# A modulation step moved, sums of squares moved between engines, and two products exchanged in a two-layer diffusion trunk

## The chip, the cores and the metric

The kernel runs on one core of a Trainium2 chip, all in float32. The metric is the device time of one execution in microseconds (us). Five engines run their own instruction streams and meet at semaphores: TensorE (PE: matmuls and transposes, results in PSUM), VectorE (DVE), ScalarE (ACT), GpSimd (POOL, which doesn't touch PSUM here) and SyncE (SP), which only issues DMAs. ACT and POOL issue some DMAs too.

## The reference

One inference step of DEPTH = 2 layers for 512 latent tokens and 128 context tokens, D = 1024. Layer 0 mixes by latent attention and retention, layer 1 by a Conformer convolution; each is followed by a mixture of 32 experts (top 2). Cut to what the change touches:

```
mp, ms = modulation(c_ctx, ...), modulation(c, ...)      # silu(cond) @ ada_w + ada_b, six parts of 1024
# layer 0, end:
xp = xp + mp[5] * hier_moe(hp, ...)                      # 128 context tokens
xs = xs + ms[5] * hier_moe(hs, ...)                      # 512 latent tokens
# layer 1, start:
h = modulate(rms_norm(x, norm_mix), m[0], m[1])          # x * rsqrt(mean(x^2) + eps), then scale and shift
a, g = split(h @ w_in);  u = a * sigmoid(g)
u = depthwise_conv(u, dw, dw_b)                          # 31 taps
u = silu(layer_norm(u, ln_g, ln_b))
x = x + m[2] * (u @ w_out)                               # the output product: 1024 x 1024 weights, 640 tokens
```

## The kernel before, in words

The residual stream lies transposed in SBUF as `xT` (128 partitions x 8 row blocks x 640 tokens). Tokens are cut in five tiles of 128 (`NT` = 5); `TILES` visits the context tile first, then the four latent ones. Nothing plans the order of work: each engine's block in the source is its queue, and semaphores (`ev(name)`) join them.

**End of layer 0 to the start of layer 1.** When the expert outputs are all in HBM (`y_done`), ACT issues five DMAs (L1672) that bring them back as `ygat`, one per tile. In the meantime TensorE multiplies the last eight blocks of modulation weights (`modulation`, L695). Its result leaves PSUM through ACT (`mod_rows(4)`), TensorE turns it in four transposes (`mod_columns(4)`, L684, bank 7), and DVE adds the bias (`mod_bias(4)`, L1754), which raises `mod_c`. These columns hold the gate and the shift that layer 1 uses after its convolution, so nothing of the stage described here reads them; TensorE waits for `mod_c` because a later step writes the same bank.

Then five tiles pass through this row of steps:

- TensorE `combine(s)` (L1201): per half of four row blocks, 4 x 2 products with diagonal weight matrices, 16 matmul instructions a half (each float32 matmul is two instructions). Two halves a tile.
- DVE `residual(s)` (L2281): four instructions a half, added to `xT`; raises `comb`. A bank comes free for `combine` after the half four before.
- ACT squares each half into `hT` (L1436).
- POOL folds the eight row blocks of squares to one in three additions (L2606), for the first four tiles.
- TensorE `tile_sum(s)`: one product with a matrix of ones (L1211), that is two instructions. For the fifth tile the eight blocks are summed by eight products instead (L1216, 16 instructions).
- ACT takes the root (L1443).
- DVE `normed_tile(s)`: reciprocal (L2290), then one product over all eight row blocks (L1754, 128x1024).

The loops of the engines set the lags: TensorE does `combine(s)`, then `tile_sum(s - 2)`; ACT squares tile s, then takes the root of s - 2; DVE does `residual(s)`, then `normed_tile(s - 3)`. After the fifth `normed_tile`, ACT and DVE apply scale and shift, and the gated input product (L1270, 64 instructions of 320 columns for each of 16 parts) begins.

**Output product of layer 1.** `project_out` computes each pair of row blocks by seven products of half size in place of eight (a Strassen scheme): products 1, 2 and 3 read inputs as they are, 5, 6, 7 and 4 read sums of them. `ORDER = (1, 5, 2, 6, 3, 7, 4)`; q = 0, 1 are two column halves of the weights, mt two output blocks in each. Each (product, mt) is a step (`out_step`, 28 a layer) of 4 matmuls, 8 instructions (L762), and raises `wo_mm`. The steps take six banks in turn, so a step waits until DVE has taken the one six before (`take`, L2080, raises `wo_ev`). Product 1 of layer 1 needs `cvn[:, 0:4]`, product 2 `cvn[:, 4:8]`; ACT writes these eight blocks in order (SiLU, L1732), and product 1 of mt 0 waits for them one by one.

The sums of the inputs (`row_sums`) are four DVE instructions over 128x1280 elements (L1754), each with both operands in SBUF, and stand on DVE ahead of every `take`. The sums of the weights are six POOL additions of 128x1024 (`weight_sums`, L2499, L2501, L2502) and, once product 2 of a q is done, one subtraction that overwrites product 2's weights (`last_sum`, L2509), which product 3 then reads.

Of the kernel before, what the change touches and what calls it, by code (L numbers as in the profile page):

```python
# [165 lines left out]
def build(nc, io):  # L166
    f = io
    ctx = ExitStack()
    with ctx:
# [220 lines left out]
        SETUP = 3  # L390
        POOLSET = SETUP + NT - 1
        TURNED = 2 + 2 * NT
# [41 lines left out]
        GATING, ROUTING = 7, 6  # L434
        ORDER = (1, 5, 2, 6, 3, 7, 4)
        SEQ = (0, 1, 4, 5, 2, 3, 6, 7)
# [4 lines left out]

        def out_step(mt, product):

            return 14 * (mt // 2) + 2 * ORDER.index(product) + mt % 2 + 1

        def out_bank(mt, product):

            return (1, 4, 3, 6, 5, 7)[(out_step(mt, product) - 1) % 6]

        def row_done(l, k):  # L450

            return 28 * l + out_step(k % 4, 3 if k < 4 else 4)
        back_full = {}
# [220 lines left out]
        def _(pe):  # L674
# [44 lines left out]
            def project_out(l, x1, x2):  # L719

                kind = ("ev_out", "od_out")[l]
                n0 = 28 * l

                def ready(mt, product):

                    q = mt // 2
                    if out_step(mt, product) > 6:
                        pe.wait_ge(ev("wo_ev"), n0 + out_step(mt, product) - 6)
                    if product in (5, 6, 7):
                        pe.wait_ge(ev("w_sum"), 8 * l + 3 * q + product - 4)  # L730
                        pe.wait_ge(ev("x_sum"), 4 * l + product - 4)
                    if product == 3:
                        pe.wait_ge(ev("w_sum"), 8 * l + 6 + q + 1)
                    if product == 4:
                        pe.wait_ge(ev("x_sum"), 4 * l + 4)
                    if l == 0:
                        if product == 1:
                            pe.wait_ge(ev("ot_v"), NT)
                        if product == 5:
                            pe.wait_ge(ev("o_c"), 6)  # L740
                        if product == 3:
                            pe.wait_ge(ev("octx_c"), 4)
                    elif product == 2:
                        pe.wait_ge(ev("mod_c"), MODC + 6)

                for q in range(2):
                    arrived((kind, q))
                    arrived((kind, 2 + q))
                    w1, w2 = out_weights(l, q), out_weights(l, 2 + q)
                    for product in ORDER:  # L750
                        for mt in (2 * q, 2 * q + 1):
                            ready(mt, product)
                            c = slice(mt % 2 * P, mt % 2 * P + P)
                            for i in range(4):
                                if l == 1 and mt == 0 and product in (1, 2):
                                    pe.wait_ge(ev("ln_sq"), KD + 1 + (0 if product == 1 else 4) + i + 1)
                                left = {1: w1[:, K1[l] + i, c], 2: w1[:, K2[l] + i, c], 3: w1[:, K2[l] + i, c],
                                        4: w2[:, K2[l] + i, c], 5: weight_sum(l, q, 0)[:, i, c],
                                        6: weight_sum(l, q, 1)[:, i, c], 7: w2[:, K1[l] + i, c]}[product]
                                right = {1: x1(i)[:, 0:SEG], 2: x2(i)[:, 0:SEG], 3: x2(i)[:, SEG:T], 4: row_sum[:, 3, i, :],  # L760
                                         5: row_sum[:, 0, i, :], 6: row_sum[:, 1, i, :], 7: row_sum[:, 2, i, :]}[product]
                                last = pe.matmul(PS[:, out_bank(mt, product), 0:SEG], left, right, start=(i == 0), stop=(i == 3))  # L762
                            last.then_inc(ev("wo_mm"), 1)

# [281 lines left out]
            def moe(l):  # L1046
# [136 lines left out]
                if l == 0:  # L1183
                    for n in range(4 * KD, 5 * KD):
                        modulation(n)
                    mod_columns(4)
                    pe.wait_ge(ev("mod_c"), MODC + 5)

# [16 lines left out]
                def tile_sum(s):  # L1205

                    if s >= 2:
                        pe.wait_ge(ev("root"), ROOT[2] + s - 1)
                    if s < NT - 1:
                        pe.wait_ge(ev("h_c"), SETUP + s + 1)  # L1210
                        last = pe.matmul(PS[:, s % 2, 0:P], ones, hT[:, 0, cols(TILES[s])], start=True, stop=True)  # L1211
                    else:
                        for k in range(KD):
                            if k % 4 == 0:
                                pe.wait_ge(ev("squared"), KD + s + 1 + k // 4)
                            last = pe.matmul(PS[:, s % 2, 0:P], ones, hT[:, k, cols(TILES[s])],  # L1216
                                             start=(k == 0), stop=(k == KD - 1))
                    last.then_inc(ev("sumsq"), 1)
# [25 lines left out]
                if l == 1:  # L1244
# [3 lines left out]
                    return  # L1248
                for s in range(NT + 2):
                    if s < NT:  # L1250
                        combine(s)
                    if s >= 2:
                        tile_sum(s - 2)

# [69 lines left out]
        def _(act):  # L1324
# [103 lines left out]
            def norm_tiles():  # L1428

                act.activation(tick[:, 3:4], eps, ACT.Sqrt)  # L1430
                for s in range(NT + 2):
                    if s < NT:
                        for half in range(2):
                            ks = slice(4 * half, 4 * half + 4)
                            act.wait_ge(ev("comb"), 2 * s + half + 1)
                            ins = act.activation(hT[:, ks, cols(TILES[s])], xT[:, ks, cols(TILES[s])], ACT.Square)  # L1436
                            if half == 1 or s == NT - 1:
                                ins.then_inc(ev("squared"), 1)
                    if s >= 2:
                        act.wait_ge(ev("sumsq"), s)  # L1440
                        if s >= 4:
                            act.wait_ge(ev("hn"), HN[2] + s - 3)
                        act.activation(PS[:, 2 + s % 2, 0:P], PS[:, s % 2, 0:P], ACT.Sqrt, bias=eps, scale=1.0 / D) \  # L1443
                            .then_inc(ev("root"), 1)
# [299 lines left out]
        def _(dve):  # L1744
# [299 lines left out]
            def add_square(l, n):  # L2044

                dve.wait_ge(ev("squared"), (KD + NT + 1) * l + n + 1)
                if n >= 2:
# [22 lines left out]
            def add_out(l):  # L2070

                def take(mt, product):

                    dve.wait_ge(ev("wo_mm"), 28 * l + out_step(mt, product))
                    if product != 1:
                        dve.wait_ge(ev("wo_ev"), 28 * l + out_step(mt, product) - 2)
                    for row, n in USES[product]:
                        m = mt + row
                        for c0, c1, who in (((0, SEG, 0),), ((SEG, SAMPLE, 0), (SAMPLE, T, 1)))[n]:
                            last = dve.scalar_tensor_tensor(  # L2080
                                out=xT[:, m, c0:c1], in0=PS[:, out_bank(mt, product), c0 - n * SEG:c1 - n * SEG],
                                scalar=modT[:, l, 16 + m, who:who + 1], in1=xT[:, m, c0:c1], op0=ALU.mult, op1=ALU.add)
                    last.then_inc(ev("wo_ev"), 1)

                for q in range(2):
                    for product in ORDER:
                        for p in range(2):
# [14 lines left out]
            def moe(l):  # L2102
# [164 lines left out]
                with dve.Fori(0, end) as n:  # L2267
                    gate_block(n)
                if l == 0:
                    mod_bias(4)  # L2270

                def residual(s):
# [44 lines left out]
                if l == 1:  # L2317
# [3 lines left out]
                    return  # L2321
                for s in range(NT + 3):
                    if s < NT:
                        residual(s)
                    if s >= 3:
                        normed_tile(s - 3)
                dve.wait_ge(ev("hn"), HN[2] + NT)
# [64 lines left out]
        def _(pool):  # L2392
# [111 lines left out]
            def last_sum(l, q):  # L2504

                a12 = out_weights(l, q)[:, K2[l]:K2[l] + 4, :]
                pool.wait_ge(ev("w_sum"), 8 * l + 6)
                pool.wait_ge(ev("wo_mm"), 28 * l + out_step(2 * q + 1, 2))
                pool.tensor_tensor(a12, a12, weight_sum(l, q, 1), ALU.subtract).then_inc(ev("w_sum"), 1)  # L2509
# [91 lines left out]
            moe(0)  # L2601
            for s in range(NT - 1):
                pool.wait_ge(ev("squared"), KD + s + 1)
                for n in (4, 2, 1):
                    t = cols(TILES[s])
                    ins = pool.tensor_tensor(hT[:, 0:n, t], hT[:, 0:n, t], hT[:, n:2 * n, t], ALU.add)  # L2606
                    if n > 1:
                        link(ins)
                ins.then_inc(ev("h_c"), 1)
            ctx_mod(2)  # L2610
# [79 lines left out]
```

## Time and profile before

| what | us |
|---|---|
| median of 3 runs | 1319.2 (1317.21 to 1320.07) |
| the profiled execution, as timed | 1319.7 |
| its span in the trace | 1317.9 |
| TensorE busy | 1185.1 (90%) |
| DVE / ACT / POOL busy | 606.3 / 380.9 / 434.0 |
| first `combine` to first gated input matmul | 721.09 to 753.45 |
| output product of layer 1, first to last matmul | 943.88 to 1007.40 |

The profile is of one execution. Times in rows are counted from the start of its span. Busy times of an engine say little about what a change is worth; the two stretches of the last lines are where the changed instructions lie.

### The profile page before, as it was taken

The numbers are of one execution on the slowest core, as the hardware profiler recorded it, in microseconds if no ns is written. First come the engines' busy times: TensorE is split into PE (matmuls) and PEld (weight loads), VectorE is DVE, ScalarE is ACT, GpSimd is POOL, SyncE is SP. The second block draws the span as 40 slices with busy tenths as digits, with TensorE's granted clock in tenths as the row PEclk, the third lists the DMA queues.
The fourth block names the chain that finished last, engine by engine and source line by source line (L and its number), as shares of the span: only waits on it lengthen the run. The fifth ranks groups of instructions, "written<-read, shape, count | busy, mean of one in ns | idle before, by whom it ended". The sixth has DMA issues, their size and how long they took to land.

```text
span 1317.9 us, 20755 instructions
## 1 busy us (share of the span) xinstructions
PE 1185.1 (90%) x6709; PEld 746.4 (57%) x6710; DVE 606.3 (46%) x1381; ACT 380.9 (29%) x786; POOL 434.0 (33%) x739
## 2 busy tenths in 40 slices
PE   6999998989999499997786799999799599999884
PEld 5566797555566455553342666666377355555442
DVE  3120344776866522221110739999785422222226
ACT  2120036655522211111110436565514111111111
POOL 0300100340000134443332449997600234444420
PEclk9999999979999799999997899999899799999997
DMA  9775550000053899999997921111763899999976
GB/s 378 267 287 215 210 178 33 3 1 1 1 101 148 349 394 422 423 423 423 424 423 302 301 81 64 64 64 33 196 203 150 316 375 397 384 422 423 422 284 271
DMA packets 107301, 324.76 MB, mean 246 GB/s; under 512 B 23029, under 2 KB 56795, under 8 KB 84707
## 3 DMA queue, kind: packets, MB, share of 16 engines
q1 hardware_dynamic: 86640, 290.38, 57.1%
q0 software_dynamic: 12464, 21.91, 4.7%
q10 hardware_dynamic: 8131, 11.59, 2.5%
q8 instruction: 41, 0.67, 0.2%
q14 instruction: 25, 0.20, 0.0%
HBM read 314.53 MB, written 27.11 MB: 259 GB/s over the span
## 4 chain that ended last, share of the span: by engine, by line
PE 59%; issue 14%; DVE 8%; DMA 7%; POOL 6%; ACT 2%; SPq 2%; POOLq 1%; ACTq 1%; DVEq 0%
PE PS L1270 10%; PE PS L806 9%; PE PS L762 9%; PE PS L1127 8%; PE PS L1149 4%; PE PS L996 3%; POOL arena L2536 2%; PE PS L695 2%; DMA arena<-in_moe_w_down 2%; DVE arena L1754 2%; DMA arena<-in_moe_w_up 2%; DMA ring<-in_ada_w 2%; PE PS L1112 2%; DVE scratch L1754 2%; PE PS L1009 1%
## 5 line engine op out<-in xcount | busy, mean ns | idle before, releaser
L1754 DVE TENSOR_TENSOR arena<-arena,PS 128x128 f32<-128x128 f32 (+3 forms) x109 | 40.2, 385 | 288.8 <-ACT arena L1645 287.6
L1270 PE MATMUL PS<-arena,ring 128*128 128x320 f32 x512 | 141.8, 438 | 7.8 <-issue 6.5
L1127 PE MATMUL PS<-ring,arena 128*64 128x256 f32 x1088 | 131.2, 393 | 16.4 <-DMA ring<-in_moe_w_up 14.7
L2623 POOL TENSOR_TENSOR arena<-arena 128x655 f32<-128x655 f32 x91 | 129.7, 1425 | 42.8 <-ACT arena L1717 30.0
L806 PE MATMUL PS<-ring,arena 128*128 128x256 f32 (+1 forms) x640 | 141.9, 375 | 1.7 <-ACT arena L1457 1.7
L1127 PE MATMUL PS<-arena 128*64 128x256 f32 x1120 | 130.6, 383 | 13.9 <-DMA arena<-in_moe_w_up 12.8
L806 PEld LDWEIGHTS PS<-ring,arena 128*128 128x128 f32 x640 | 115.6, 192 | 28.8 <-issue 14.5
L762 PE MATMUL PS<-arena,ring 128*128 128x320 f32 x448 | 123.8, 439 | 5.1 <-ACT arena L1732 4.8
L1270 PEld LDWEIGHTS PS<-arena,ring 128*128 128x128 f32 x512 | 98.0, 193 | 51.3 <-issue 12.7
L2355 DVE SCALAR_TENSOR_TENSOR PS<-arena,vecT,PS 128x655 f32<-128x655 f32 x124 | 112.1, 904 | 4.2
L1127 PEld LDWEIGHTS PS<-ring,arena 128*64 128x64 f32 x1088 | 77.9, 140 | 59.4 <-DMA ring<-in_moe_w_up 13.3
L762 PEld LDWEIGHTS PS<-arena,ring 128*128 128x128 f32 x448 | 86.3, 193 | 42.6 <-issue 7.6
L1127 PEld LDWEIGHTS PS<-arena 128*64 128x64 f32 x1120 | 78.1, 137 | 55.5 <-DMA arena<-in_moe_w_up 10.9
L1717 ACT ACTIVATE arena<-arena,vecT 128x655 f32<-128x655 f32 x99 | 80.1, 839 | 52.9 <-POOL arena L2623 35.1
L1645 ACT ACTIVATE arena<-PS 128x128 f32<-128x128 f32 x69 | 19.1, 277 | 256.4 <-PE PS L1127 256.4
L1656 ACT ACTIVATE arena<-PS 128x512 f32 x61 | 36.4, 597 | 152.7 <-PE PS L1149 152.7
L2527 POOL TENSOR_TENSOR pool_tick<-cst 128x1 f32<-128x1 f32 x120 | 22.1, 184 | 176.5 <-ACT arena L1656 175.1
L2080 DVE SCALAR_TENSOR_TENSOR xT<-PS,modT,xT 128x320 f32<-128x320 f32 (+2 forms) x176 | 63.1, 421 | 35.6 <-PE PS L762 35.5
L1149 PE MATMUL PS<-arena 128*64 128x512 f32 x280 | 67.8, 605 | 1.5 <-ACT arena L1656 0.8
L1112 PE MATMUL PS<-cst,arena 128*128 128x128 f32 x284 | 53.9, 313 | 16.4 <-DVE arena L2236 16.4
L2536 POOL DMA_INDIRECT arena<-h_rows,gather_col x56 | 59.2, 1058 | 27.6 <-issue 27.6
L2541 POOL DMA_INDIRECT y_rows<-arena,scatter_col x56 | 56.9, 1017 | 32.4 <-issue 32.4
(363 smaller groups left out, 1613.7 us busy)
## 6 DMA issues: line engine op xcount, KB each, us to landing
arena<-in_moe_w_up SPq DMA_DIRECT2D x64, 1024.0 KB, 19.2
ring<-in_moe_w_up SPq DMA_DIRECT2D x64, 1024.0 KB, 15.0
ring<-in_ada_w SPq DMA_DIRECT2D x46, 1024.0 KB, 10.9
arena<-in_moe_w_down SPq DMA_DIRECT2D x32, 1024.0 KB, 20.0
ring<-in_moe_w_down SPq DMA_DIRECT2D x32, 1024.0 KB, 16.3
arena<-y_rows ACTq DMA_DIRECT2D x10, 1024.0 KB, 9.5
ring<-in_od_w_in SPq DMA_DIRECT2D x16, 512.0 KB, 6.2
ring<-in_ev_w_in SPq DMA_DIRECT2D x7, 1024.0 KB, 15.8
```

What stands on the lines that cost most here:

```text
L762: last = pe.matmul(PS[:, out_bank(mt, product), 0:SEG], left, right, start=(i == 0), stop=(i == 3))
L806: last = pe.matmul(z_bank(i)[:, 0:n], hT[:, k, t * P:t * P + P], w[:, k, 0:n], start=(k == 0), stop=(k == KD - 1))
L1112: last = pe.transpose(quad(3)[:, m, :], xrow.rearrange("p (c m) -> p m c", m=4)[:, m, :], ident)
L1127: last = pe.matmul(PS[i * BLK:(i + 1) * BLK, 0, 0:2 * P].rearrange("p (a n) -> p a n", a=2), xblk[:, k, :], w[:, k % 4, :, i * P:(i + 1) * P],
L1149: last = pe.matmul(PS[c * BLK:(c + 1) * BLK, 2, :], hblk[:, i, :], w[:, i, c * 512:(c + 1) * 512], start=(i == 0), stop=(i == 1))
L1270: last = pe.matmul(PS[:, 2 * a + n, 0:SEG], w[:, k, a, :], hT[:, k, n * SEG:(n + 1) * SEG], start=(k == 0), stop=(k == KD - 1))
L1717: act.activation(dst, src, ACT.Copy, scale=tap_weight(w, j)).then_inc(ev("prod"), 1)
L1754: return dve.tensor_tensor(out, a, b, op)
L2080: last = dve.scalar_tensor_tensor(out=xT[:, m, c0:c1], in0=PS[:, out_bank(mt, product), c0 - n * SEG:c1 - n * SEG], scalar=modT[:, l, 16 + ...
L2355: dve.scalar_tensor_tensor(out=conv_acc, in0=src, scalar=tap_weight(w, j), in1=conv_acc, op0=ALU.mult, op1=ALU.add).then_inc(ev("conv_v"), 1)
L2536: pool.indirect_dma_start(land[r], None, h_rows[:, :], bass.IndirectOffsetOnAxis(ap=col, axis=0), bounds_check=2 * T - 1, oob_is_err=False ...
L2623: pool.tensor_tensor(acc, acc, prod[:, i % PRODS, :], ALU.add).then_inc(ev("conv_p"), 1)
```

## The change

Three edits. (a) `mod_columns(4)`, its wait and `mod_bias(4)` move from before `combine(0)` and `residual(0)` to behind them. (b) The POOL additions are gone; ACT announces every half of squares, and TensorE sums all five tiles by eight products each. All lags shorten by one: `tile_sum(s - 1)`, root of s - 1, `normed_tile(s - 2)`. (c) In layer 1 the order of products becomes (1, 2, 5, 6, 3, 7, 4), and for q = 0 products 1 and 2 alternate between mt 0 and 1 after each of the four matmuls. Layer 0 keeps its order. Counts of semaphores follow.

```diff
-        POOLSET = SETUP + NT - 1
+        POOLSET = SETUP
...
-        ORDER = (1, 5, 2, 6, 3, 7, 4)
+        ORDERS = ((1, 5, 2, 6, 3, 7, 4), (1, 2, 5, 6, 3, 7, 4))
...
-                    elif product == 2:
+                    elif product == 5:
                         pe.wait_ge(ev("mod_c"), MODC + 6)
...
-                    for product in ORDER:
-                        for mt in (2 * q, 2 * q + 1):
+                    for product in ORDERS[l]:
+                        pair = (2 * q, 2 * q + 1)
+                        for mt in pair:
                             ready(mt, product)
+                        by_chunk = l == 1 and q == 0 and product in (1, 2)
+                        for n in range(8):
+                            mt, i = (pair[n % 2], n // 2) if by_chunk else (pair[n // 4], n % 4)
...
                 if l == 0:
                     for n in range(4 * KD, 5 * KD):
                         modulation(n)
-                    mod_columns(4)
-                    pe.wait_ge(ev("mod_c"), MODC + 5)
...
-                    if s < NT - 1:
-                        pe.wait_ge(ev("h_c"), SETUP + s + 1)
-                        last = pe.matmul(PS[:, s % 2, 0:P], ones, hT[:, 0, cols(TILES[s])], start=True, stop=True)
-                    else:
-                        for k in range(KD):
-                            if k % 4 == 0:
-                                pe.wait_ge(ev("squared"), KD + s + 1 + k // 4)
-                            last = pe.matmul(PS[:, s % 2, 0:P], ones, hT[:, k, cols(TILES[s])],
-                                             start=(k == 0), stop=(k == KD - 1))
+                    for k in range(KD):
+                        if k % 4 == 0:
+                            pe.wait_ge(ev("squared"), KD + 2 * s + 1 + k // 4)
+                        last = pe.matmul(PS[:, s % 2, 0:P], ones, hT[:, k, cols(TILES[s])],
+                                         start=(k == 0), stop=(k == KD - 1))
...
-                for s in range(NT + 2):
+                for s in range(NT + 1):
                     if s < NT:
                         combine(s)
-                    if s >= 2:
-                        tile_sum(s - 2)
+                    if s == 0:
+                        mod_columns(4)
+                        pe.wait_ge(ev("mod_c"), MODC + 5)
+                    if s >= 1:
+                        tile_sum(s - 1)
...
-                if l == 0:
-                    mod_bias(4)
...
-                for s in range(NT + 3):
+                for s in range(NT + 2):
                     if s < NT:
                         residual(s)
-                    if s >= 3:
-                        normed_tile(s - 3)
+                    if s == 0:
+                        mod_bias(4)
+                    if s >= 2:
+                        normed_tile(s - 2)
...
-                pool.wait_ge(ev("wo_mm"), 28 * l + out_step(2 * q + 1, 2))
+                pool.wait_ge(ev("wo_mm"), 28 * l + out_step(l, 2 * q + 1, 2))
...
-            for s in range(NT - 1):
-                pool.wait_ge(ev("squared"), KD + s + 1)
-                for n in (4, 2, 1):
-                    t = cols(TILES[s])
-                    ins = pool.tensor_tensor(hT[:, 0:n, t], hT[:, 0:n, t], hT[:, n:2 * n, t], ALU.add)
-                    if n > 1:
-                        link(ins)
-                ins.then_inc(ev("h_c"), 1)
             ctx_mod(2)
```

## Rows read from the trace of the kernel before

**Rows 1.** The page: busy time and share of the span of each engine.
```profile
PE 1185.1 (90%) x6709; PEld 746.4 (57%) x6710; DVE 606.3 (46%) x1381; ACT 380.9 (29%) x786; POOL 434.0 (33%) x739
```

**Rows 2.** Chain that ended last: start us, us, what. "issue": no releaser shown.
```profile
719.65 0.20 DVE modT L1754
...
721.09 13.74 PE PS L1201 x96
...
746.98 6.47 issue
753.45 19.55 PE PS L1270 x64
...
774.12 17.46 PE PS L1270 x64
...
951.17 56.23 PE PS L762 x208
```

**Rows 3.** First of the five DMA issues of L1672, issue to landing.
```profile
L1672 ACTq DMA_DIRECT2D arena<-y_rows x1: 392/392/392, 714.1 to 714.1; - x1
...
DMA to landing us min/median/max: 6.9/6.9/6.9
```

**Rows 4.** Timeline 727 to 753: start, length, instruction, [idle before <- releaser].
```profile
727.72 1.12 DVE L2281 SCALAR_TENSOR_TENSOR xT<-PS,modT,xT 128x128 f32<-128x128 f32 x4 [1.71 <-PE PS L1201]
...
729.50 1.13 DVE L2281 SCALAR_TENSOR_TENSOR xT<-PS,modT,xT 128x128 f32<-128x128 f32 x4 [0.66 <-PE PS L1201]
...
734.23 0.63 ACT L1436 ACTIVATE arena<-xT 128x512 f32<-128x512 f32 x1 [1.15 <-DVE xT L2281]
...
734.66 0.39 PE L1211 MATMUL PS<-arena,cst 128*128 128x128 f32 x2
...
736.56 0.32 ACT L1443 ACTIVATE PS<-PS,cst 128x128 f32<-128x128 f32 x1
...
744.92 2.05 PE L1216 MATMUL PS<-arena,cst 128*128 128x128 f32 x16 [1.18 <-ACT PS L1443]
...
748.15 0.96 DVE L2290 RECIPROCAL PS<-PS 128x128 f32<-128x128 f32 x1
...
750.28 0.96 DVE L2290 RECIPROCAL PS<-PS 128x128 f32<-128x128 f32 x1
751.28 1.22 DVE L1754 TENSOR_TENSOR arena<-xT,PS 128x1024 f32<-128x1024 f32 x1
```

**Rows 5.** Windows: length, busy PE, PEld, DVE, ACT, POOL, then PEclk, DMA.
```profile
749.00:751.00 2.00, 0.00 (x0) 0.00 (x0) 1.97 (x3) 0.00 (x0) 0.00 (x0) 0.95 1.03 294
751.00:753.40 2.40, 0.00 (x0) 0.00 (x0) 2.33 (x4) 0.87 (x2) 0.00 (x0) 0.50 1.14 342
...
942.00:943.80 1.80, 0.00 (x0) 0.00 (x0) 1.80 (x5) 0.98 (x2) 1.80 (x2) 0.50 1.02 419
```

**Rows 6.** Timeline of TensorE and POOL at the output product.
```profile
943.88 6.97 PE L762 MATMUL PS<-arena,ring 128*128 128x320 f32 x16 [4.82 <-ACT arena L1732]
...
949.64 3.59 POOL L2502 TENSOR_TENSOR ring<-ring 128x1024 f32<-128x1024 f32 x1
...
960.17 2.36 POOL L2509 TENSOR_TENSOR ring<-ring 128x1024 f32<-128x1024 f32 x1 [6.94 <-PE PS L762]
```

**Rows 7.** Timeline of DVE there: the four row sums, then the first pieces taken.
```profile
948.90 2.12 DVE L1754 TENSOR_TENSOR arena<-arena 128x1280 f32<-128x1280 f32 x1
951.13 3.45 DVE L1754 TENSOR_TENSOR arena<-arena 128x1280 f32<-128x1280 f32 x1
954.50 1.48 DVE L1754 TENSOR_TENSOR arena<-arena 128x1280 f32<-128x1280 f32 x1
955.90 1.48 DVE L1754 TENSOR_TENSOR arena<-arena 128x1280 f32<-128x1280 f32 x1
957.31 0.54 DVE L2080 SCALAR_TENSOR_TENSOR xT<-PS,modT,xT 128x320 f32<-128x320 f32 x1
...
959.39 0.53 DVE L2080 SCALAR_TENSOR_TENSOR xT<-PS,modT,xT 128x320 f32<-128x320 f32 x1
```

More of the change, by code:

```diff
@@ L440, in build, with out_step, out_bank @@
                 3: ((0, 1),), 7: ((4, 0), (4, 1)), 4: ((4, 0),)}
[L442 to L448, printed above, removed]
+        def out_step(l, mt, product):
+            return 14 * (mt // 2) + 2 * ORDERS[l].index(product) + mt % 2 + 1
+        def out_bank(l, mt, product):
+            return (1, 4, 3, 6, 5, 7)[(out_step(l, mt, product) - 1) % 6]
         def row_done(l, k):
-            return 28 * l + out_step(k % 4, 3 if k < 4 else 4)
+            return 28 * l + out_step(l, k % 4, 3 if k < 4 else 4)
         back_full = {}
@@ L726, in ready @@
                     q = mt // 2
-                    if out_step(mt, product) > 6:
-                        pe.wait_ge(ev("wo_ev"), n0 + out_step(mt, product) - 6)
+                    if out_step(l, mt, product) > 6:
+                        pe.wait_ge(ev("wo_ev"), n0 + out_step(l, mt, product) - 6)
                     if product in (5, 6, 7):
@@ L753, in project_out @@
                             c = slice(mt % 2 * P, mt % 2 * P + P)
[L754 to L762, printed above, removed]
@@ L763, in project_out @@
-                            last.then_inc(ev("wo_mm"), 1)
+                            if l == 1 and mt == 0 and product in (1, 2):
+                                pe.wait_ge(ev("ln_sq"), KD + 1 + (0 if product == 1 else 4) + i + 1)
+                            left = {1: w1[:, K1[l] + i, c], 2: w1[:, K2[l] + i, c], 3: w1[:, K2[l] + i, c],
+                                    4: w2[:, K2[l] + i, c], 5: weight_sum(l, q, 0)[:, i, c],
+                                    6: weight_sum(l, q, 1)[:, i, c], 7: w2[:, K1[l] + i, c]}[product]
@@ L765, in _ @@
+                            right = {1: x1(i)[:, 0:SEG], 2: x2(i)[:, 0:SEG], 3: x2(i)[:, SEG:T], 4: row_sum[:, 3, i, :],
+                                     5: row_sum[:, 0, i, :], 6: row_sum[:, 1, i, :], 7: row_sum[:, 2, i, :]}[product]
+                            last = pe.matmul(PS[:, out_bank(l, mt, product), 0:SEG], left, right, start=(i == 0), stop=(i == 3))
+                            if i == 3:
+                                last.then_inc(ev("wo_mm"), 1)
             pe.wait_ge(ev("params_in"), 16 * NPARAM)
@@ L1430, in norm_tiles @@
                 act.activation(tick[:, 3:4], eps, ACT.Sqrt)
-                for s in range(NT + 2):
+                for s in range(NT + 1):
                     if s < NT:
@@ L1435, in norm_tiles @@
                             act.wait_ge(ev("comb"), 2 * s + half + 1)
[L1436 to L1443, printed above, removed]
+                            act.activation(hT[:, ks, cols(TILES[s])], xT[:, ks, cols(TILES[s])], ACT.Square) \
+                                .then_inc(ev("squared"), 1)
+                    if s >= 1:
+                        b = (s - 1) % 2
+                        act.wait_ge(ev("sumsq"), s + 1)
+                        if s >= 3:
+                            act.wait_ge(ev("hn"), HN[2] + s - 2)
+                        act.activation(PS[:, 2 + b, 0:P], PS[:, b, 0:P], ACT.Sqrt, bias=eps, scale=1.0 / D) \
                             .then_inc(ev("root"), 1)
@@ L2044, in add_square @@
             def add_square(l, n):
-                dve.wait_ge(ev("squared"), (KD + NT + 1) * l + n + 1)
+                dve.wait_ge(ev("squared"), (KD + 2 * NT) * l + n + 1)
                 if n >= 2:
@@ L2072, in take @@
                 def take(mt, product):
-                    dve.wait_ge(ev("wo_mm"), 28 * l + out_step(mt, product))
+                    dve.wait_ge(ev("wo_mm"), 28 * l + out_step(l, mt, product))
                     if product != 1:
-                        dve.wait_ge(ev("wo_ev"), 28 * l + out_step(mt, product) - 2)
+                        dve.wait_ge(ev("wo_ev"), 28 * l + out_step(l, mt, product) - 2)
                     for row, n in USES[product]:
@@ L2080, in take @@
                             last = dve.scalar_tensor_tensor(
-                                out=xT[:, m, c0:c1], in0=PS[:, out_bank(mt, product), c0 - n * SEG:c1 - n * SEG],
+                                out=xT[:, m, c0:c1], in0=PS[:, out_bank(l, mt, product), c0 - n * SEG:c1 - n * SEG],
                                 scalar=modT[:, l, 16 + m, who:who + 1], in1=xT[:, m, c0:c1], op0=ALU.mult, op1=ALU.add)
@@ L2085, in add_out @@
                 for q in range(2):
-                    for product in ORDER:
+                    for product in ORDERS[l]:
                         for p in range(2):
```

## The prediction

> **What bounds the kernel now.** I read the page first: TensorE is busy for 90% of the span [rows 1], so work added to it tends to cost, and work taken off other engines tends to give nothing. Then the chain of waits, to see what ends last in the two stretches that the change touches [rows 2]; then their timelines [rows 4, 6, 7], the landing of one DMA [rows 3], and the granted clock at idle gaps [rows 5].
>
> Two things are to be seen in the chain. From 721.09 TensorE's `combine` carries it (96 instructions without a break), and later the end of the stage hangs on DVE's last `normed_tile`, at 751.28 + 1.22 = 752.50; the gated input product starts 0.95 us later, at 753.45. And from 951.17 the output product runs for 56.23 us without a break: 208 instructions, 0.270 us each, 2.16 us per step of eight. So each microsecond by which these two starts move is a microsecond of the kernel; nothing after them shows slack of its own, since each later stage begins with what these release.
>
> **(a) The modulation columns.** Before, the transposes and the bias end at 719.65 + 0.20 = 719.85 [rows 2]. `combine(0)` starts at 721.09. It also needs the first tile of expert outputs: issued at 714.1, landed 6.9 us later, at 721.0 [rows 3]. So the DMA released it, and the columns lay in its shadow for nothing. Moved, they let nothing start earlier. And they gain a price: TensorE now stands after `combine(0)` until DVE has done both halves of `residual(0)` (727.72 + 1.12 = 728.84) [rows 4] and the bias, 0.20, so until about 729.1. Queued behind the wait is `combine(1)`, whose first half before was ready for DVE at 729.50, 1.78 after the last of `combine(0)`; it therefore started about 727.5. Cost: +1.6 us at this point.
>
> **(b) The sums of squares.** A tile sum was two instructions: 0.39 us recorded, about 0.22 of TensorE's time (0.11 an instruction, since a half of 16 takes 1.78) [rows 4]. It becomes 16: the fifth tile's took 2.05 from first start to last end, of which about 1.8 occupy the engine and 0.2 are the last one's way through it. I price each at 1.8. What POOL did was hidden, and an engine that is no bound gives nothing back.
>
> Walk with these prices, 3.58 for a `combine`, 1.1 for half a `residual`, 0.6 for a square, 0.32 for a root, 2.13 for a `normed_tile` (748.15 to 750.28):
>
> - TensorE: `combine(1)` 729.1 to 732.7; sum 0 to 734.5; `combine(2)` to 738.1; sum 1 to 739.9; `combine(3)` to 743.45; sum 2 to 745.25; `combine(4)` to 748.8; sum 3 to 750.6.
> - Each sum finds its squares ready, and DVE's `normed_tile(0)` and `(1)` fit into its idle time (739.4 to 741.5, 744.8 to 746.9) but for sum 4: half a `residual` ends at 750.15, its square at 750.8, the sum runs 750.95 to 752.8, its root is there at 753.3.
> - DVE after 750.15: three `normed_tile`, the last to 750.15 + 3 x 2.13 = 756.5. The last root, 753.3, comes before the third of them starts (754.4), so DVE sets the end.
>
> The same walk with the old order gives 752.6 against 752.50 seen, so its error is small. The stage ends at 756.5 in place of 752.5: **+4.0 us**. Split: +1.6 from (a), +3 x 1.8 for sums 0 to 2 that now stand ahead of the end of `combine(4)`, -2 x 0.22 for those that stood there, and -2.6 because after `combine(4)` DVE has 7.7 us left instead of 10.3 (one `normed_tile` more has been done by then, and its residual isn't late). Bounds: at 1.7 a sum, +3.7; at 2.05, the whole recorded stretch, +4.7. If the wait of (a) were hidden, 1.6 less: +2.4.
>
> The clock adds to this. TensorE idled 6.47 us before the gated input product; the granted clock fell from 1.00 to 0.50, that is from 2.4 to 1.2 GHz, some 3.8 us into the gap, and the first 64 instructions then took 19.55 us where the next took 17.46 [rows 2, 5]: 2.1 us. Now TensorE idles from 753.0 to 757.4, 4.4 us. Before the output product it idled 4.82, and the clock was down at the start there too [rows 5, 6]. So I keep that loss, term zero; if the clock stayed up, -2.1.
>
> **(c) The order of products.** The first step starts with the first SiLU block either way, at 943.88. The 16 instructions of product 1 took 6.97 us, the first half of them at 1.2 GHz, with two short waits for blocks that alternating between mt hides: about 0.1. Product 5 then waited for the first row sum until 951.17; product 2 would follow at about 950.3 without it. Gain so far 0.9, and steps 3 to 6 then end at 950.3 + 4 x 2.16 = 958.9.
>
> But step 7 needs the bank of step 1, which DVE takes after its row sums: 957.31 to about 959.4 (the next take starts at 959.39) [rows 7]. Before, TensorE came there at 951.17 + 4 x 2.16 = 959.8, just behind. Now it comes at 958.9 and stands until 959.45. Of the gain 0.35 us is left, even with DVE's work unchanged.
>
> And DVE's work changes. The same row sum takes 1.48 us alone, but 2.12 and 3.45 while POOL runs its weight sums; POOL's own L2502 takes 3.59 against 2.36 for the same shape [rows 6, 7]. The excess, 0.64 + 1.97 on DVE, 1.23 on POOL, fits engines that take turns: L2502 stood until the first row sum ended at 951.02, then ran to 953.23, and the second row sum, issued at 951.13, only then did its 1.4. Takes read PSUM and keep 0.53 beside POOL's L2509 at 960.17. The change moves L2509 forward, because product 2 of mt 1 is step 4 instead of 6: done at 954.8, POOL ready at 955.0 instead of 960.17. At that time DVE is in the third row sum (954.50 to 955.98), with the fourth queued. If POOL goes in between, the fourth waits 2.36 us, ends at 959.7, the first take (2.08) at 961.8, and step 7 starts at 961.85 instead of 959.8: **+2.0 us**. Later takes keep up (2.08 against TensorE's 2.16 a step; product 2's are shorter). If the fourth row sum goes first, POOL waits, at no cost (product 3 reads L2509's result only from 963), and (c) is -0.35. Both ends are open; between them I take +2.0, because at 951 to 953 POOL did get in between two row sums, though these were also apart by a semaphore.
>
> The Trainium skill ("SBUF — State Buffer", section "SBUF: two separate sides") says that a VectorE instruction with two SBUF inputs and a GpSimd instruction that reads SBUF exclude each other, and that the one which starts first holds the ports for its whole length. The 3.45 and 3.59 above agree. By it L2509, waiting since 955.0, would go ahead of a fourth row sum issued at 955.9, which is the +2.0; a mere sharing of bandwidth would give some 1 us.
>
> **Sum.** 1319.7 (the profiled execution as timed; its span is 1317.9) + 4.0 + 2.0 = 1325.7. The median of the runs is 0.5 below that execution: 1325.2. I call 0.2%, 2.6 us, what a measurement can tell from no change.
>
> **The rivals.**
> 1. *No collision*: POOL's subtraction waits or comes beside nothing. For it: 0.9 us of delay in product 2 is enough, and back-to-back row sums may leave no opening. Time 1325.2 - 2.35 = 1322.9.
> 2. *The clock stays up*: the gap before the gated input product is 4.4 instead of 6.47 us. Against it: the gap of 4.82. Time 1325.2 - 2.1 = 1323.1; with rival 1, 1320.8.
> 3. *The wait of (a) is hidden*, because `combine(1)` has less to do than the walk has it or DVE is quicker: 1325.2 - 1.6 = 1323.6.
> 4. The other side, *sums at almost no cost*: eight products with the same ones keep their weights, or slip into openings between `combine` instructions. Then a sum costs 0.2 and the walk gives about +0.2 for the stage instead of +4.0. With (c) at +2.0 the kernel is at 1321.4, no change; with (c) at -0.35 at 1319. It decides from 0.6 us a sum downward. Against it: the fifth tile's 2.05 for 16, with a weight load beside each.
>
> **How the numbers follow.** Chances: forecast 0.43, rival 1 0.26, rival 2 0.10 (with or without 1), rival 3 0.08, rival 4 0.08, dearer than the forecast 0.05. The range reaches from 1321.0, which leaves out most of rival 4 and the pair of 1 and 2, to 1327.5, which is a sum at 2.05, a half-clock start up to 1 us longer and the spread of the runs (1.5 us each way). Slower needs more than 1321.8: forecast, the dearer cases, most of rivals 1 and 3, half of 2: 0.78. Same: 0.18. Faster: what rival 4 could give with every other term favourable: 0.04.
>
> **What would show it.** In the profile after: `combine(0)` still at 721.1 behind the landing; a gap of about 1 us on TensorE after its last half, released by DVE's bias; five groups of 16 sums, 1.8 to 2.0 us each; the last `normed_tile` ending near 756.5; L2509 at about 956 and the fourth row sum at over 3 us; a wait of TensorE for L2080 at step 7 of up to 3 us. I am wrong if `combine(0)` starts earlier, if the sums are short, or if the gated input product begins before 755.

## The result and the profile after

| what | before | changed |
|---|---|---|
| median, us | 1319.2 (5 runs, 1317.21 to 1320.37) | 1328.72 (5 runs, 1327.71 to 1332.2) |
| ratio | | 1.0075, 95% interval 1.0057 to 1.0093 |
| profiled execution, as timed | 1319.7 | 1330.18 |
| span | 1317.9 | 1328.3 |

The change costs 9.5 us. The direction was forecast (6.0 us, 1325.2), the size was not: 1328.72 lies above the range, which ended at 1327.5.

The page, its line on the engines, to set beside [rows 1]:

```profile
PE 1192.4 (90%) x6765; PEld 751.4 (57%) x6766; DVE 609.0 (46%) x1381; ACT 381.7 (29%) x786; POOL 426.2 (32%) x727
```

The chain that ended last, after the change, to set beside [rows 2]:

```profile
728.87 3.84 PE PS L1203 x32
732.71 1.79 PE PS L1214 x16
734.50 3.57 PE PS L1203 x32
...
752.36 4.93 issue
757.29 19.11 PE PS L1271 x64
...
954.58 8.40 DVE arena L1755 x3
962.98 2.15 DVE xT L2081 x7
965.13 0.32 issue
965.45 1.72 DVE xT L2081 x5
967.16 0.35 issue
967.52 49.94 PE PS L765 x176
```

Two things are new. In the first stretch the sums (L1214, 1.79 us each) have joined the chain. In the second the chain runs over three row sums and then twelve more DVE instructions, two `take`s of six, before the output product goes on: where [rows 2] has one piece of 208 instructions, there are 176, behind a gap.

**The first stretch**, timeline after the change:

```profile
722.09 5.46 PE L1203 MATMUL PS<-scratch,arena 128*128 128x128 f32 x32 [2.01 <-DMA arena<-y_rows]
...
727.39 0.60 PE L684 MATMUL PS<-cst,arena 128*128 128x128 f32 x4
727.59 1.13 DVE L2279 SCALAR_TENSOR_TENSOR xT<-PS,modT,xT 128x128 f32<-128x128 f32 x4 [1.40 <-PE PS L1203]
728.63 0.18 DVE L1755 TENSOR_TENSOR modT<-PS,vecT 128x32 f32<-128x32 f32 x1
728.87 3.84 PE L1203 MATMUL PS<-scratch,arena 128*128 128x128 f32 x32 [0.88 <-DVE modT L1755]
...
748.62 3.74 PE L1214 MATMUL PS<-arena,cst 128*128 128x128 f32 x32
...
755.12 1.22 DVE L1755 TENSOR_TENSOR arena<-xT,PS 128x1024 f32<-128x1024 f32 x1
```

The first `combine` is now shown as waiting for the DMA, as the landing in [rows 3] said it had been all along; then TensorE stands 0.88 us for DVE's bias. From DVE's second half residual (727.59) to the end of the last normed tile (756.34) it is 28.75 us; before, 727.72 to 752.50, 24.78 [rows 4]. That is +3.97, where the walk had +4.0. The first `combine` itself ran 1.1 us quicker (first matmul to second residual 5.50 against 6.63), since more of it ran at 2.4 GHz, so the whole stretch from first `combine` to gated input grew by 2.84 only. This is not an effect of the change: below, E1 and E9 have the code of before in this stretch, and their first `combine` took 5.48 and 5.29. In these two the length counted from the second half residual is 25.27 and 25.14, for the first sum then comes early enough to meet ACT and POOL late. So the agreement with +4.0 is partly luck of the clock: against the same code at the same speed of the first `combine` the stretch grew by about 3.5.

**The second stretch.** DVE, in narrow windows of the timeline, and then TensorE and POOL:

```profile
952.35 2.13 DVE L1755 TENSOR_TENSOR arena<-arena 128x1280 f32<-128x1280 f32 x1
954.58 3.44 DVE L1755 TENSOR_TENSOR arena<-arena 128x1280 f32<-128x1280 f32 x1
957.95 1.48 DVE L1755 TENSOR_TENSOR arena<-arena 128x1280 f32<-128x1280 f32 x1
959.35 3.63 DVE L1755 TENSOR_TENSOR arena<-arena 128x1280 f32<-128x1280 f32 x1
962.91 0.54 DVE L2081 SCALAR_TENSOR_TENSOR xT<-PS,modT,xT 128x320 f32<-128x320 f32 x1
...
947.32 15.34 PE L765 MATMUL PS<-arena,ring 128*128 128x320 f32 x48 [4.82 <-ACT arena L1733]
...
958.51 3.13 POOL L2509 TENSOR_TENSOR ring<-ring 128x1024 f32<-128x1024 f32 x1 [1.83 <-PE PS L765]
...
967.52 49.94 PE L765 MATMUL PS<-arena,ring 128*128 128x320 f32 x176 [4.85 <-DVE xT L2081]
```

Against [rows 7], the first three row sums are the same to 0.01 us and the fourth takes 3.63 in place of 1.48: POOL's subtraction, shown from 958.51, got in ahead of it. But the six steps (48 instructions) end at 962.7, and step 7 starts not after the first take (about 965.0) but at 967.52, after the second. TensorE stood 4.85 us. The windows (columns as in [rows 5]) show what that did:

```profile
962.70:965.70 3.00, 0.00 (x0) 0.00 (x0) 3.00 (x9) 0.00 (x0) 0.00 (x0) 0.95 0.47 96
965.70:967.50 1.80, 0.00 (x0) 0.01 (x1) 1.80 (x6) 0.00 (x0) 0.00 (x0) 0.50 1.04 360
967.50:972.10 4.60, 4.58 (x9) 3.03 (x10) 2.90 (x10) 0.00 (x0) 0.00 (x0) 0.50 0.98 369
972.10:974.00 1.90, 1.90 (x9) 1.33 (x8) 1.72 (x5) 0.00 (x0) 0.00 (x0) 0.97 0.99 366
```

The granted clock fell to 1.2 GHz in the gap and stayed there for the first 4.6 us of work. From its first instruction to the first of the next step, step 7 took 4.40 us, where a step at full clock takes 2.15.

The account of the profiled execution, 1319.7 to 1330.18: +1.0 ahead of the first `combine`, by work that the change doesn't touch; +2.84 to the gated input product; -0.44 in that product's first 64 instructions (19.11 against 19.55); 0.0 in the convolution between; +6.61 from the first matmul of the output product to the first of the router (947.32 to 1017.38, before 943.88 to 1007.33); the rest 0.5.

### The profile page after: what moved, and what is told of

The parts are those of the page before. It is cut to its first block, busy times and chain, and to the rows that moved or that the text cites. A ratio compares the mean times of both kernels' runs of the same rounds, so it can differ in the third digit from the quotient of the medians.

```text
span 1328.3 us, 20870 instructions
## 1 busy us (share of the span) xinstructions
PE 1192.4 (90%) x6765; PEld 751.4 (57%) x6766; DVE 609.0 (46%) x1381; ACT 381.7 (29%) x786; POOL 426.2 (32%) x727
## 4 chain that ended last, share of the span: by engine, by line
PE 62%; DMA 11%; SPq 10%; DVE 9%; issue 4%; ACT 2%; POOL 2%; ACTq 0%; DVEq 0%; POOLq 0%
PE PS L1131 10%; PE PS L1271 10%; PE PS L810 9%; PE PS L765 8%; PE PS L1153 5%; SPq L594 5%; DMA arena<-in_moe_w_up 4%; SPq L597 3%; PE PS L1000 3%; DVE arena L1755 2%; PE PS L695 2%; PE PS L1116 2%; DMA arena<-in_moe_w_down 2%; DMA ring<-in_moe_w_up 2%; DMA ring<-in_ada_w 2%
## 5 line engine op out<-in xcount | busy, mean ns | idle before, releaser
L810 PEld LDWEIGHTS PS<-ring,arena 128*128 128x128 f32 x640 | 116.2, 193 | 30.2 <-issue 15.3
```

Of the source, the lines that this page charges most:

```text
L810: last = pe.matmul(z_bank(i)[:, 0:n], hT[:, k, t * P:t * P + P], w[:, k, 0:n], start=(k == 0), stop=(k == KD - 1))
```

## The experiments

Kernels that are equal up to layer 0's output product reached it anywhere from 362.4 to 368.6 us in their profiles, and most of that spread, 5.4 us, is there some 125 us after the start. So a single profile's span says little, and the two stretches are read by their own length: from DVE's second half residual to the end of the last normed tile ("stage"), and from the first matmul of layer 1's output product to the first of its router ("product"). "Step 7" is the start of that product's 49th matmul instruction, counted from its first, where TensorE stood ahead of it. The last three columns are us, each from one profile. The ratio is to the kernel before on the same chip. E10 leaves out part of each sum and computes other values, so its ratio says nothing.

| kernel | ratio (95%) | stage | product | step 7 |
|---|---|---|---|---|
| before | | 24.78 | 63.45 | |
| before, again | one run | 24.79 | 65.72 | |
| changed | 1.0075 (1.0057 to 1.0093) | 28.75 | 70.06 | 20.20 |
| changed, again | one run | 30.15 | 70.30 | 20.17 |
| E1 order only | 1.0055 (1.0037 to 1.0073) | 25.27 | 70.70 | 20.18 |
| E2 (a) and (b) only | 1.0034 (1.0020 to 1.0048) | 28.75 | 63.43 | |
| E3 waits per step | 1.0053 (1.0038 to 1.0068) | 28.75 | 67.06 | 17.80 |
| E4 POOL late | 1.0065 (1.0047 to 1.0082) | 28.75 | 67.27 | 18.04 |
| E5 both repairs | 1.0039 (1.0024 to 1.0054) | 28.95 | 63.21 | |
| E6 columns back | 1.0077 (1.0056 to 1.0098) | 27.63 | 70.15 | 20.18 |
| E7 columns only | 1.0004 (0.9991 to 1.0018) | 26.37 | 63.44 | |
| E9 sums deferred | 0.9998 (0.9985 to 1.0012) | 25.13 | 63.26 | |
| E10 two of eight blocks | 0.9979 (0.9963 to 0.9995) | 25.20 | 63.42 | |
| E11 short lags | 1.0039 (1.0020 to 1.0057) | 26.63 | 63.44 | |

The theory after the result: (c) costs by three links, namely POOL's subtraction ahead of the fourth row sum; a wait for two takes in place of one; and the clock lost by the gap that these make. The second link is in the diff. Before, each step's waits stood ahead of its own matmuls. Now both waits of a pair stand ahead of the first:

```diff
-                        for mt in (2 * q, 2 * q + 1):
+                        for mt in pair:
                             ready(mt, product)
```

so step 7 also waits for the bank of step 8, that is for DVE to have taken step 2.

**E1 and E2, the halves of the change.** E1 is the kernel before with `ORDERS` and the new loop of `project_out`; E2 is the changed kernel with the old ones.

```diff
 # E2, on the changed kernel
-        ORDERS = ((1, 5, 2, 6, 3, 7, 4), (1, 2, 5, 6, 3, 7, 4))
+        ORDERS = ((1, 5, 2, 6, 3, 7, 4), (1, 5, 2, 6, 3, 7, 4))
...
-                        for mt in pair:
+                        for mt in (2 * q, 2 * q + 1):
                             ready(mt, product)
-                        by_chunk = l == 1 and q == 0 and product in (1, 2)
...
```

> The kernel before with the new order of products alone (c), layer 0 waiting in pairs too as in the changed kernel. Theory of three links: the fourth row sum takes over 3 us beside POOL's subtraction; step 7 then waits for two taken steps, because both waits of a pair stand ahead of its first matmul; TensorE idles 4 to 5 us there and goes on at 1.2 GHz for about 4 us. Together +6 to +7 us against before (about 1326). Rival A, the alternation between two banks or the order itself is slow: the output product longer with no idle time on TensorE. Rival B, the two edits (a) and (b) carry the loss: +0 to +2 here.

> Edits (a) and (b) alone, output product as before. Walk of the prediction: normed tiles end 4.0 us later after the first combine than before, kernel +3.5 to +4.5 us (about 1323), output product unchanged at 56.2 us from its 17th instruction on. If (c) was harmless and (a) and (b) carry the loss: +9.

E1 costs 0.55% of 1317.8, 7.2 us, and its product is 7.25 longer, with TensorE idle 4.19 us ahead of step 7; E2 costs 0.34%, 4.5 us, with its stage 3.97 longer and its product unchanged. Rival B of E1 is out, and so is the notion that (c) was harmless. Rival A is out too: the loss is idle time and half clock, while the first 48 instructions take 15.3 us (changed, E3) to 16.0 (E1, E4) with the alternation and 16.1 without it (E2, a short wait for the first row sum included); the time depends on when the clock rises. The new loop hoists the waits in layer 0 as well, and there it costs nothing: layer 0's output product takes 60.49 us in every one of these profiles, old loop or new, without a stop of TensorE.

**E3 and E4, one link each.**

```diff
 # E3
-                        for mt in pair:
-                            ready(mt, product)
                         by_chunk = l == 1 and q == 0 and product in (1, 2)
                         for n in range(8):
                             mt, i = (pair[n % 2], n // 2) if by_chunk else (pair[n // 4], n % 4)
+                            if i == 0:
+                                ready(mt, product)
 # E4, POOL's last_sum
                 pool.wait_ge(ev("wo_mm"), 28 * l + out_step(l, 2 * q + 1, 2))
+                if l == 1 and q == 0:
+                    pool.wait_ge(ev("x_sum"), 4 * l + 4)
```

> The changed kernel with each step's waits just ahead of its own first matmul, as before the change. Three links: step 7 starts one taken step (about 2.1 us) and some tenths earlier, TensorE idles about 2.5 us instead of 4.85 and keeps 2.4 GHz, which gives 2.2 us more: 4 to 5 us faster than the changed kernel (about 1324). If the paired waits don't matter: no difference.

> The changed kernel with POOL's first subtraction of layer 1 held back until all four row sums are done. Three links: the fourth row sum takes 1.5 instead of 3.6 us, takes start 2.1 us earlier, TensorE's idle time is about 2.7 us and the clock stays at 2.4 GHz, so again 4 to 5 us faster than the changed kernel. If POOL and DVE only happened to be slow together: the fourth row sum stays at 3.6 us and nothing is gained.

Step 7 comes 2.40 us earlier in E3 (20.20 to 17.80) and 2.16 earlier in E4 (to 18.04). In E4 the fourth row sum is back at 1.48, with POOL started behind it (timeline of DVE in a narrow window, then of POOL):

```profile
962.32 1.48 DVE L1755 TENSOR_TENSOR arena<-arena 128x1280 f32<-128x1280 f32 x1
...
963.97 2.36 POOL L2511 TENSOR_TENSOR ring<-ring 128x1024 f32<-128x1024 f32 x1 [4.32 <-DVE arena L1755]
```

So both first links hold, at their size. The forecast of 4 to 5 us was missed in both: the products are shorter by 3.0 and 2.8 only, because the clock fell although TensorE stood just 2.45 and 2.02 us. E3, the gap and the work behind it, first in the timeline and then in windows:

```profile
966.24 8.96 PE L765 MATMUL PS<-arena,ring 128*128 128x320 f32 x26 [2.45 <-DVE xT L2081]
...
963.80:966.20 2.40, 0.00 (x0) 0.00 (x0) 2.40 (x8) 0.00 (x0) 0.00 (x0) 1.00 0.45 133
966.20:966.80 0.60, 0.56 (x2) 0.40 (x3) 0.60 (x2) 0.00 (x0) 0.00 (x0) 0.76 1.07 437
966.80:970.00 3.20, 3.20 (x8) 2.00 (x7) 3.20 (x10) 0.00 (x0) 0.00 (x0) 0.51 1.04 379
970.00:972.00 2.00, 2.00 (x9) 1.44 (x8) 2.00 (x8) 0.00 (x0) 0.00 (x0) 1.00 0.95 391
```

The clock was still up when work went on, and fell just after (in E4 1.4 us after). The kernel's times alone would not tell E3 and E4 from the changed kernel, since their intervals overlap; the traces do.

**E5, both repairs.** Both edits above.

> The changed kernel with both repairs: waits per step, and POOL's first subtraction behind the four row sums. If the three links are all of (c): step 7 starts 15.6 us after the first matmul of the output product (15.9 before the change, 20.2 in the changed kernel), TensorE idles 0.3 us there, the clock stays at 2.4 GHz, the product takes 63.2 us (63.5 before, 70.1 changed), and the kernel stands where (a) and (b) alone put it, +4 to +5 us against before. If something else in the new order costs: 65 us or more.

```profile
947.66 63.28 PE L765 MATMUL PS<-arena,ring 128*128 128x320 f32 x224 [4.82 <-ACT arena L1733]
```

All 224 instructions in one piece, product 63.21, as expected: the three links are all of (c). What was not foreseen is that the 0.3 us at step 7 doesn't show either: DVE's first take ended just in time, since here the clock rose later and TensorE came there later. The kernel (+0.39%) stands with E2 (+0.34%), where (a) and (b) put it.

**E6 and E7, the modulation columns.** E6 moves `mod_columns(4)`, its wait and `mod_bias(4)` back in the changed kernel; E7 moves them behind the first tile in the kernel before.

```diff
 # E7
-                    mod_columns(4)
-                    pe.wait_ge(ev("mod_c"), MODC + 5)
...
                     if s < NT:
                         combine(s)
+                    if s == 0:
+                        mod_columns(4)
+                        pe.wait_ge(ev("mod_c"), MODC + 5)
                     if s >= 2:
                         tile_sum(s - 2)
...
```

> The changed kernel with edit (a) undone: modulation columns ahead of the first combine again. Walk: the second tile's combine starts 1.6 us earlier, first combine unchanged (it waits for the landing), the last normed tile ends 1.6 us earlier after the first combine; kernel about 1.6 us under the changed one. If the wait is hidden: no difference in the stage. If TensorE's columns did hold back the first combine: no gain, or a loss of 1 us.

> Edit (a) alone on the kernel before. Walk: stage +1.6 us from first combine to last normed tile, kernel +1.6 us. If the columns were on the path before: 1 us faster.

E7's stage is 1.59 longer than that of the kernel before, as the walk had it, but only 1.10 longer than that of E1, whose first `combine` took as long (5.48 in E1, 5.51 in E7). TensorE stands 0.88 us for DVE's bias there too; the kernel's time doesn't tell it from nothing (+0.5 us, interval -1.2 to +2.4). E6's stage shrinks by 1.12, not 1.6. Its first sum now comes early enough to wait for ACT, which was issuing DMAs for the router's weights until 728.9 and then loading a table. The changed kernel's second profile shows the same limit, harder: its first `combine` ran at full clock throughout, so the first sum stood 1.13 us for the squares, and the stage, counted from DVE, is 30.15. That is 1.4 over the 28.75 expected of it, where 0.8 had been allowed.

```profile
731.70 1.49 PE L1214 MATMUL PS<-arena,cst 128*128 128x128 f32 x11 [1.13 <-ACT arena L1437]
```

E6's kernel time (+0.77%) is no better than the changed kernel's; 1.1 us can't be seen in it.

**E10, the price of a sum.** On E2, and only two of the eight row blocks are summed.

```diff
-                    for k in range(KD):
-                        if k % 4 == 0:
-                            pe.wait_ge(ev("squared"), KD + 2 * s + 1 + k // 4)
+                    for k in (0, 4):
+                        pe.wait_ge(ev("squared"), KD + 2 * s + 1 + k // 4)
...
```

> Edits (a) and (b) alone, with each sum of squares over two of the eight row blocks only (4 matmul instructions instead of 16; the other six blocks are left out, so values after it, and with them the routing of layer 1's experts, differ: the stage is to be read, not the kernel's time). TensorE's time for the sums sets (b): the walk with 0.45 us a sum ends the stage 3.5 us earlier than with 1.8, so about 25.3 us from the second half residual to the last normed tile instead of 28.75. Rival, the path from squares over sum and root to DVE sets it: at most the latency of one sum, 1.4 us, is gained.

Stage 25.20, the walk had 25.3: 3.55 us less for 12 instructions less in each sum. TensorE's own time sets (b). Rival 4 of the prediction, that eight products go at almost no cost, is out by this: a stage of 25.2 is what a cheap sum would have given, and the changed kernel has 28.75.

**E11, short lags with POOL's additions.** The kernel before with `s - 1` for `s - 2` on TensorE and ACT, and `s - 2` for `s - 3` on DVE.

```diff
-                for s in range(NT + 2):
+                for s in range(NT + 1):
                     if s < NT:
                         combine(s)
-                    if s >= 2:
-                        tile_sum(s - 2)
+                    if s >= 1:
+                        tile_sum(s - 1)
...
```

> The kernel before with the lags shortened by one on TensorE, ACT and DVE, and POOL's additions kept. Walk: each sum on TensorE now waits for POOL's three additions, stage +1.0 us. If short lags were what costs in (b): +2.3 us or more. If they give something: less than before.

Stage +1.85 (+1.36 against E1), between the +1.0 of the walk and the +2.3 of its rival: the first sum stood for POOL, longer than the walk had it, because ACT's squares came late here as well.

```profile
737.22 0.49 PE L1211 MATMUL PS<-arena,cst 128*128 128x128 f32 x2 [2.77 <-POOL arena L2607]
```

So short lags lose while the sums wait for POOL. Without that wait they do gain: E10, with short lags and sums of four instructions, has a stage of 25.20, and E7, with long lags, sums of two and edit (a) like it, has 26.37. The full sums of the changed kernel then cost more than this. The kernel's +0.39% (5.1 us) is more than the 1.85 of its stage; its profile was 5.7 us late by layer 0's output product already, and whether that belongs to this kernel is open.

**E9, the order without its costs.** The kernel before with the new order, waits per step as in E3, and the third and fourth row sum moved behind the takes of products 1 and 2.

```diff
                         for p in range(2):
                             take(2 * q + p, product)
+                        if l == 1 and q == 0 and product == 2:
+                            later_sums(l, cvn[:, 0:4, :], cvn[:, 4:8, :])
```

> The kernel before with the new order of products, waits per step, and the third and fourth row sum moved behind DVE's takes of products 1 and 2, so that neither TensorE's step 7 nor POOL's subtraction meets them. By the three links nothing holds TensorE: product in 62.6 us, 0.9 us under before, kernel 0.9 us faster, which is within what can be measured. If row sums behind the takes starve product 5's or 6's takes: TensorE idles at steps 9 to 12 and the product takes 64 us or more.

TensorE doesn't stop once in the product. It is 63.26 instead of 62.6. The clock rose only 5.7 us after the start here (4.9 before); 0.8 us more at half clock make some 0.4 us of it, an estimate. The rest is that product 2 can follow product 1 less early than the 0.9 us of the prediction. Ratio 0.9998: no loss, and no gain that can be measured. Against E1's 1.0055 the intervals are apart, so it is not the order of products that costs 7 us but what was tied to it. It is also the best complete version among the runs, and it equals the kernel before.

**The two kernels again.**

> The kernel before, once more with a profile. Stage and output product as in the first profile within 0.5 us (24.8 and 63.5); what comes ahead of layer 0's output product may differ by some us, as it has between kernels that are equal up to there.

> The changed kernel, once more with a profile. Stage 28.75 and output product 70 us again, within 0.8 for where the clock steps fall; the time of the first layer 0 output matmul free between 362 and 367 us.

The stage of the kernel before came back at 24.79, its product at 65.72, 2.3 longer, where 0.5 had been allowed. The timeline of DVE and POOL has the cause:

```profile
946.19 2.37 DVE L1754 TENSOR_TENSOR delta<-modT 128x8 f32<-128x8 f32 x1
...
946.18 2.36 POOL L2499 TENSOR_TENSOR ring<-ring 128x1024 f32<-128x1024 f32 x1
```

An addition of eight elements a row, which has two SBUF inputs, took 2.37 us here. In each of the thirteen other profiles of this document it took 0.15, though the same POOL addition started within 0.01 us of it there as well. In those thirteen POOL's start is at most 3 ns ahead of DVE's, here it is 9 ns ahead. The next normalized blocks, their SiLU and the rest of product 1 waited behind it. So the kernel before lost 2.3 us by the same exclusion in one of its two profiled executions, and nothing in the code keeps the changed kernel from it. The changed kernel's product was 70.30, within the 0.8.

## Why the prediction was wrong

**Where it held.** The DMA's landing, not the columns, released the first `combine`. Edit (a) costs 1.1 to 1.6 (E6, E7; forecast 1.6), the sums about 1.8 each, the stage +3.5 to +4.0 (forecast +4.0; 28.75 in the changed kernel's first profile and in E2, E3 and E4, against 24.78 to 25.27 for the code of before). E10 shows the same of the sum's size. The first links of (c) held too: product 5's wait gone, POOL's subtraction moved beside the row sums and taking the port ahead of the fourth, 3.63 us, takes 2.15 later. The +2.0 forecast for (c) put step 7 at 17.97 after the first matmul; E3, where only the missed link is undone, has 17.80. The rule of the Trainium skill ("SBUF — State Buffer", section "SBUF: two separate sides") that the engine which comes first holds the ports for its whole instruction went the right way where the trace of before could not decide.

**The step that failed** is "step 7 needs the bank of step 1". In the changed code it needs the banks of steps 1 and 2, because `ready` is called for both mt before the first matmul. I read the diff for the order of the matmuls and not for where its waits had gone. That adds 2.4 us (E3). "Later takes keep up" was true, and no help: TensorE now asks for them a step earlier.

**The term left at nothing** is the clock behind this gap. The prediction priced the clock only at the gap before the gated input product. It had TensorE stop ahead of step 7 from 958.9 to 961.85, 3 us in the middle of 2.4 GHz work, and then go on at full clock. Stops of 2.0 and 2.45 us there already cost another 1.8 us (E3, E4: 49.3 and 49.2 us from step 7 to the router; 47.5 before), and those of 4.85 and 4.2 cost 2.4 and 3.05 (changed kernel, E1). So (c) is +6.61: +4.2 until step 7 and +2.4 behind it, where I had +2.0 and 0. A smaller error lies in the gain: product 2 was to start 0.9 us earlier. It started 0.7 earlier in the changed kernel, where the clock rose early, and 0.1 in E1 and E9, where it rose late.

**The rivals.** No collision: out by the 3.63 and by E4. The clock stays up before the gated input product: out, its first 64 instructions took 19.11. The wait of (a) hidden: out by the 0.88 us that TensorE stands and by the stages of E6 and E7, though a third of the 1.6 can be hidden. Sums at almost no cost: out by E10. None of them was on the side where the error lay; "dearer than the forecast" had 0.05 and deserved a mechanism.

**What stays open.** The sum of both stretches is 4.0 + 6.6 = 10.6 (10.1 with a stage of +3.5) against 9.5 of the medians, whose interval is 7.5 to 12.3; E1 and E2 add up to 11.7. That is within the noise and was not followed further. Why executions of equal code reach layer 0's output product up to 6 us apart was not tried, nor why the clock falls after one stop of 2 to 2.5 us and not after another.

## What to carry to other kernels

When a loop is rewritten to interleave two steps, list for each wait which matmul it now stands in front of: a wait hoisted over a pair turns a ring of six banks into one of five for the first of the pair. Price a stop of TensorE as the stop plus what the clock may take afterwards, also for stops of 2 us. And before moving a GpSimd instruction earlier, look which VectorE instructions with two SBUF inputs run at its new place, small ones included; E4 shows that holding it back by one semaphore wait brings the row sum back to 1.48 us.

## What the runs showed of the hardware

- The granted clock fell after gaps of 2.45 and 2.02 us of TensorE (E3, E4), and in both it did so after work had gone on, for 3.4 and 3.3 us. It doesn't always: in the changed kernel's second profile TensorE stood 2.55 us ahead of the first `combine` and 0.88 us behind it, and the granted clock was 1.00 throughout, from 718 to 752.
- A VectorE addition of 128x8 elements with two SBUF inputs took 2.37 us when a GpSimd addition of 2.36 had started 9 ns ahead of it; in the thirteen other profiles, GpSimd at most 3 ns ahead, it took 0.15. Instructions with one input in PSUM keep their time beside GpSimd (0.53 to 0.54 for 128x320 with GpSimd busy and without).
- GpSimd got in between two VectorE instructions that stood one behind the other, where the semaphore between them (for the second row sum, done at 958.02) held nothing up any more: third row sum 957.95 to 959.43, the fourth issued at 959.35, and yet it ended 1.3 us after GpSimd's instruction did (958.51 + 3.13 = 961.64).
